# One quarter of a weight chunk moved between the two tiles of x, and one rounding cut into halves, at the start of a four-block network

## The reference

```
h   = rmsnorm(x, g)                       # x * rsqrt(mean(x*x) + 1e-6) * g
bcv = h @ w_in                            # w_in: 1024 x 3072
b, c, v = split(bcv, 3)
x   = x + (b * causal_dwconv(c * v, w_conv)) @ w_out
x   = x + conv_ffn(rmsnorm(x, g2), w_up, w_conv2, w_down)
```

## Time and profile before

| | us |
|---|---|
| median of 3 runs (1203.61 to 1203.86) | 1203.73 |
| the profiled execution's own time | 1203.73 |
| its span in the trace | 1202.4 |
| PE busy in the span | 1192.5 (99%) |
| DVE busy | 886.3 (74%) |
| ACT busy | 654.6 (54%) |

### The profile page before, as it was taken

How to read it: one execution, slowest core, us unless ns; L and a number is a source line. 1 busy time by engine, 2 the same in 40 slices (tenths; PEclk the granted TensorE clock), 3 DMA queues, 4 the chain that set the end, 5 groups by cost and what they waited for, 6 DMA issues and landing times.

```text
span 1202.4 us, 16515 instructions
## 1 busy us (share of the span) xinstructions
PE 1192.5 (99%) x6611; PEld 1025.3 (85%) x6611; DVE 886.3 (74%) x1221; ACT 654.6 (54%) x859; POOL 52.6 (4%) x75
## 2 busy tenths in 40 slices
PE   9999999999999999999999999999999999999997
PEld 8888888888777888888899888888889977888886
DVE  6977989847686798884687887776467668777744
ACT  6545666634566666663488635444327774544430
POOL 0000000000000000000005110000012001000000
PEclk9999999999999999999999999999999999999999
DMA  9755555564434455556442556555526433755630
GB/s 358 248 206 193 172 179 193 187 219 174 190 117 137 185 183 180 198 207 213 156 136 106 207 190 234 194 191 198 173 91 229 176 140 103 254 203 176 196 120 35
DMA packets 32653, 217.80 MB, mean 181 GB/s; under 512 B 3761, under 2 KB 4033, under 8 KB 8001
## 3 DMA queue, kind: packets, MB, share of 16 engines
q1 hardware_dynamic: 30704, 210.39, 49.6%
q0 software_dynamic: 1728, 6.29, 1.6%
q10 hardware_dynamic: 144, 0.07, 0.0%
HBM read 215.67 MB, written 1.05 MB: 180 GB/s over the span
## 4 chain that ended last, share of the span: by engine, by line
PE 98%; DVE 1%; DMA 1%; issue 0%; ACT 0%; POOL 0%; SPq 0%; DVEq 0%
PE ps L953 42%; PE ps L883 24%; PE ps L889 14%; PE ps L891 4%; PE ps L905 2%; PE ps L901 2%; PE ps L902 2%; PE ps L994 1%; PE ps L1022 1%; PE ps L1004 1%; PE ps L967 1%; PE ps L1086 1%; DMA t<-in_wts 1%; DVE t L1589 0%; PE ps L1032 0%; PE ps L1071 0%
## 5 line engine op out<-in xcount | busy, mean ns | idle before, releaser
L953 PE MATMUL ps<-t,t 128*128 128x512 f32 (+3 forms) x2328 | 538.0, 387 | 0.0
L1532 DVE TENSOR_TENSOR t<-t,t 128x2048 fp32r<-128x2048 f32 (+3 forms) x200 | 447.8, 2251 | 98.5 <-PE ps L953 86.9
L953 PEld LDWEIGHTS ps<-t,t 128*128 128x128 f32 x2328 | 423.1, 188 | 81.9 <-issue 2.0
L1195 ACT CAST t<-t 128x2048 fp32r<-128x2048 f32 (+3 forms) x200 | 374.2, 1883 | 198.3 <-PE ps L953 105.5
L883 PE MATMUL ps<-t,t 128*128 128x512 f32 x1274 | 305.8, 390 | 0.0
L883 PEld LDWEIGHTS ps<-t,t 128*128 128x128 f32 x1274 | 238.8, 188 | 51.3
L889 PEld LDWEIGHTS ps<-t,t 128*128 128x128 f32 x1456 | 187.2, 191 | 7.5
L889 PE MATMUL ps<-t,t 128*128 128x256 f32 x1456 | 189.5, 283 | 0.0
L1653 DVE TENSOR_REDUCE t<-ps 128x512 f32<-128x1024 f32 x40 | 48.9, 1224 | 44.4 <-PE ps L891 44.4
L1606 DVE SCALAR_TENSOR_TENSOR t<-t,t,t 128x254 f32<-128x254 f32 (+1 forms) x176 | 73.2, 478 | 10.2 <-ACT t L1212 10.2
L1252 ACT CAST t<-t 128x512 fp32r<-128x512 f32 x44 | 27.2, 619 | 91.2 <-DVE t L1637 91.2
(11 more groups left out here) (213 smaller groups left out, 841.9 us busy)
## 6 DMA issues: line engine op xcount, KB each, us to landing
t<-in_wts SPq DMA_DIRECT2D x192, 1024.0 KB, 4.9
t<-in_rows POOLq DMA_DIRECT2D x12, 512.0 KB, 4.3
t<-in_wts SPq DMA_DIRECT2D x4, 528.0 KB, 3.9
t<-in_wts SPq DMA_DIRECT2D x2, 768.0 KB, 4.6
t<-in_wts SPq DMA_DIRECT2D x2, 592.0 KB, 4.1
t<-in_x_in SPq DMA_DIRECT2D x2, 512.0 KB, 4.2
out<-t SPq DMA_DIRECT2D x4, 256.0 KB, 2.0
t<-in_wts SPq DMA_DIRECT2D x2, 256.0 KB, 6.4
```

The costliest lines, as they stand in the source:

```text
L953: ins = mm(ps[:, t_bank(stage, t, j), 0:c1 - c0], a, w[:, k, c0:c1], start=kt == 0 and part == 0, stop=kt == KTS[stage] - 1 and part == 2)
L1195: copy(wh[:, k, 0:w], wraw[:, r, 0:w]).then_inc(s_hi, 1)
L1532: tt(wl[:, k, 0:w], wraw[:, r, 0:w], wh[:, h, 0:w].bitcast(F32), ALU.subtract).then_inc(s_lo, 1)
```

## The change

Two edits at the start of the kernel.

1. SP issues the first quarter of chunk 0 between the two tiles of x instead of behind them. The other transfers keep their order.
2. ACT rounds chunk 1 in two casts of 128 x 1024 in place of one of 128 x 2048: first the columns of K slices 4 to 7, which raises a new semaphore, then those of slices 0 to 3, which raises the one that all chunks use. PE's first full block waits for the new semaphore before its first matmul, and for the old one before slice 0.

```diff
-    s_hi, s_lo = sem("s_weights_hi"), sem("s_weights_lo")
+    s_hi, s_lo, s_hi1 = sem("s_weights_hi"), sem("s_weights_lo"), sem("s_second_weights_half_hi")
...
             if blk == 0:
-                pe.wait_ge(*((s_hi, split_at(i)) if stage in WIDE else (s_lo, split_at(i))))
+                if (stage, n) == ("sc", 1):
+                    pe.wait_ge(s_hi1, 1)
+                else:
+                    pe.wait_ge(*((s_hi, split_at(i)) if stage in WIDE else (s_lo, split_at(i))))
...
                     for kt in order[:7]:
                         pe.wait_ge(*x_ready(b, kt))
+                        if (stage, n, kt) == ("sc", 1, 0):
+                            pe.wait_ge(s_hi, split_at(i))
...
-        def first_hi():
-            sl = slice(CW // 2, CW)
-            act.wait_ge(s_raw[0], 16)
-            copy(wh[:, 0, sl], wraw[:, 0, sl]).then_inc(s_hi, 1)
+        def first_hi(i):
+            sl, other = slice(CW // 2, CW), slice(0, CW // 2)
+            act.wait_ge(s_raw[i], 16)
+            copy(wh[:, i, sl], wraw[:, i, sl]).then_inc(s_hi1 if i else s_hi, 1)
+            if i:
+                copy(wh[:, i, other], wraw[:, i, other]).then_inc(s_hi, 1)
...
-                if k[0] == 0:
-                    first_hi()
+                if k[0] < 2:
+                    first_hi(k[0])
...
         dma(X[:, 0, :], x_in[0, tok(0), :]).then_inc(s_x[0], 16)
+        dma(wraw[:, 0, 0:512], wts[0, :, 0:512]).then_inc(s_first[0], 16)
         dma(X[:, 1, :], x_in[0, tok(1), :]).then_inc(s_x[1], 16)
-        for c0, c1, done in ((0, 512, s_first[0]), (512, 1024, s_first[1]), (1024, CW, s_raw[0])):
+        for c0, c1, done in ((512, 1024, s_first[1]), (1024, CW, s_raw[0])):
             dma(wraw[:, 0, c0:c1], wts[0, :, c0:c1]).then_inc(done, 16)
```

## The result

| | median us | lowest to highest | runs |
|---|---|---|---|
| before | 1203.79 | 1203.47 to 1204.01 | 17 |
| changed | 1206.71 | 1205.12 to 1207.87 | 17 |

The ratio is 1.0022, with a 95% interval of 1.0015 to 1.0028: 2.9 us slower, outside the range that was forecast. The spread matters as much as the median. Before, all runs lie within 0.54 us. The changed kernel has five runs at 1205.12 to 1205.29 and twelve at 1206.4 to 1207.9. The profiled run, at 1205.16, is one of the five. So its trace shows the part of the loss that is always there, and a second part, some 1.5 us more, has to be found elsewhere. The mean granted clock of the runs points the same way: 0.998 to 0.999 in the five, 0.995 to 0.998 in the twelve.

What follows compares the result with a forecast made beforehand. PE, busy 99%, was taken as the bound, through its first real matmul at 8.09 us. 1203.73 us, plus 1.0 for the transfer order and 0 for the halved rounding, gave 1204.7; range 1203.3 to 1205.2.

Steps and rivals of the forecast that it cites:

- The bound: PE, busy 99% of the span: whatever moves its first real matmul at 8.09 us moves the end by as much.
- The late tile: At the kernel's start, tile 1 of x lands at 7.0 to 8.0 us behind the first quarter; PE starts 1.0 late.
- The likeliest case: The slow stretch in 5 to 8 us moves with the first quarter ahead of tile 1; chance 0.52, time 1204.7 us.
- The upper end: Tile 1 is last of three transfers through at 7.95 us, so PE starts at 9.45, a loss of 1.36.
- The lower end: Three transfers through near 6.7 us by bytes, plus 0.55 to landing: tile 1 at 7.25, PE 0.7 late.
- The 1.5 us from tile 1's landing to PE's start: Before line 916: 1.45 us from tile 1's landing until x is ready, 1.5 with the semaphore.
- Rival A: At the start, the first quarter costs tile 1 only 0.62 us; PE starts at 7.9, time 1203.5; chance 0.26.
- The step on why the first quarter was slow: In 5 to 8 us, about 1.2 us lost to that transfer itself: first weight read, 2 KB pieces from 8 KB rows.
- rival B: PE's longer early gap drops the clock to 1.2 GHz, doubling line 916's 3.69 us: 1208.4 us; chance 0.06.
- The halves: Chunk 1's rounding in two casts before the first full block: worth 0, within 0.2 us gain or loss.

Runs made afterwards that it cites:

- PE held back: Kernel before, transfers in old order, with PE made to wait for the first quarter before turning tile 1: 1206.71 us, ratio 1.0024.
- the small early transfer: Kernel before plus a transfer of 64 bytes from each of chunk 0's 128 rows, ahead on ACT's queue: 1204.49 us, ratio 1.0006.

## Why the prediction was wrong

**The bound was right.** All of the change's effect came through the start of the first real matmul. Behind it everything moved by the same amount (1.47 us at line 921, 1.50 at the full block), and in the profiled run the later 1190 us added nothing: the span grew by the same 1.5.

**The late tile was right, its size just beyond the far end.** The likeliest case was that the hole moves with the first quarter, and it did. I took 1.0 us as the middle of 0.7 and 1.36; it was 1.47. By itself that makes 1205.2, the upper edge of the range, and the five quick runs and the run with the gap filled (1205.22) lie there. The upper end, "when all three are through", was the good rule: before, the three transfers were through at 7.95, now at 8.08. The lower end, a count of bytes and 0.55 us of lag, did not hold: by the same count over the changed kernel's rates the three were through near 6.9 and tile 1 would have landed near 7.5, but it landed at 8.08. The 1.5 us from tile 1's landing to PE's start held: 1.48 here and in the run with contiguous copies. Rival A (tile 1 at 6.4) is what happens with contiguous rows, or nearly: 6.85. The step on why the first quarter was slow named two causes in one breath, the first read of the weights and pieces out of longer rows. Neither is enough alone: whole rows read first have no hole, and the second quarter, in the same short pieces but behind the first, lands at full rate. The traces fit the two together.

The Trainium skill, "DMA: Bandwidth & Descriptors", section "Anatomy of one DMA", lets the time of a transfer grow with bytes over 436 GB/s, fitted for transfers that GpSimd issues; by it an estimate for 256 KB is 0.60 us. The contiguous copy, issued by SP, came near it: in the run with the copies in the old order, tile 1 landed at 5.98 and the first quarter at 6.65, 0.7 us apart. The sliced one took 2.2 us.

**The step that failed is the clock.** I had it as rival B, outside the sum and the range, with a chance of 0.06, because the column read 1.00 around a gap of 1.2 us, and priced it all or nothing at 3.7 us, by doubling line 916. By the times it came in twelve of seventeen runs, and it cost 1.5 us in the median, 2.7 at most. The price was too high because the low stretch covers only part of line 916: in the run with the order alone it had begun near 8.5 and ended near 12.0, 2.2 us into that line, and half of 2.2, 1.1 us, is about what the line lost (4.77 against 3.72). And the chance was far too low. It rested on the one gap of today, and on "this trace shows no such drop", which was a misreading: the same trace shows one at its end, where PE's last matmul ends at 1195.6 and the column reads

```profile
1199.00:1200.00 1.00, 0.00 (x0) 0.00 (x0) 1.00 (x2) 0.00 (x0) 0.00 (x0) 0.56 0.00 0
```

The new gap on PE was 2.2 us in the two traces where the clock fell, twice the old one, and stands ahead of one short burst of transposes. Of the 34 runs in which tile 1 was turned late (the changed kernel, the order alone, PE held back) 28 lie above 1206.2, so the chance should have been near that of the late tile itself. Together, 1.4 + 1.5 = 2.9 us.

The Trainium skill, "TensorE: Matmul & The Clock Gate", Part 1, has PE fall to half its clock by idleness. In the traces of the order alone and of PE held back it did, to 0.50 of full speed; in the trace of the small early transfer a gap of 1.91 us brought no fall.

**The halves were right:** nothing in three settings. In the changed kernel the two casts took 1.98 us from 13.85 to 15.83, and PE came at 16.13.

## What to carry to other kernels

- Price a wait on PE early in a kernel twice: what it delays, and what the clock then takes. A few matmuls of zeros in the gap (here twelve) take the second part away, 1.5 us here.
- When a transfer is put ahead of another, charge the one behind with the time that the first one takes in the trace, not with its bytes. If that time is far above the bytes' (here 2.2 us for 256 KB), look at the shape of its rows first: laid out contiguously the same bytes took 0.7. This kernel showed it at its first read of the weights only.
- A spread of the runs that grows from 0.5 to 2.7 us is itself a finding, and one profile shows only one of its cases.

## What the runs showed of the hardware

- Pieces of 2 KB out of rows 8 KB apart, as the first read of the weights, passed in stages of 117 to 264 GB/s and landed 2.2 us behind the transfer ahead of them. The same bytes as 2 KB rows side by side, or as part of whole rows of 8 KB, passed in stages of 344 to 442. Pieces of 4 KB out of 8 KB lay between (209 to 340). Pieces of 2 KB behind such a first read landed 0.65 us after it, which is 400 GB/s. What in the memory does it was not tried, nor whether it happens later in a kernel.
- The granted clock reads 1.00 from the first us of every trace, yet the first fifteen matmuls of zeros take 0.24 us each there and 0.14 each later on, and tile 0's eight transposes take 1.25, 1.78 or 1.97 us where they take 1.09 at full speed. So the column does not show the lower level before its first change; the durations do. How late the rise comes differs from trace to trace; in kernels that wait for x it moves the start of line 916 by some tenths or more (7.53, 7.71 and 8.26 us in three traces with contiguous copies, where 7.3 was expected).
- At 1.2 GHz three matmuls of line 916 were in progress in a stage of 1 us, against six or seven at 2.4 GHz (stage 10 to 11 us of the order alone; stages 9 to 11 of the kernel with all of chunk 0 in one piece).
- The clock can fall after PE has taken up work again: in the order alone PE began the transposes of tile 1 at 8.20, and the fall came near 8.5, in the middle of them.
